# A two-layer transformer block on one core: normed rows for the expert gather, a new order of the last expert loads, and first slots that hold one contraction step

## The reference, cut to what matters

```python
def chunk(t):                                   # t: 128 tokens x 1024, already rmsnorm(x, g)
    grp_p = softmax(t @ w_grp + b_grp)          # 4 groups of 8 experts, best group
    e_p = softmax(logits of that group)         # best two experts in it
    combine = one_hot(expert) * weights         # tokens x 32
    a = einsum('cd,edf->cef', t, w_gate)
    u = einsum('cd,edf->cef', t, w_up)
    hid = silu(a) * u * combine[..., None]
    return einsum('cef,efd->cd', hid, w_down)
```

## Time and profile before

| | us |
|---|---|
| median of 3 runs | 1060.23 (1059.67 to 1060.28) |
| the profiled execution's own time | 1059.21 |
| its span, from first to last instruction | 1057.4 |
| PE busy | 1009.9 (96%) |
| DVE busy | 286.1 (27%) |
| ACT busy | 207.1 (20%) |
| HBM read | 288.44 MB, 275 GB/s over the span |

### The profile page before, as it was taken

One profiled execution on the slowest core, in us unless ns is written; L12 is line 12 of the kernel. 1 busy time (PEld: TensorE's weight loads), 2 busy tenths in 40 slices (PEclk: granted clock), 3 DMA queues, 4 the chain that ended last, 5 costly groups with the idle time before them and its releaser, 6 DMA issues. The chain is left out here.

```text
span 1057.4 us, 14177 instructions
## 1 busy us (share of the span) xinstructions
PE 1009.9 (96%) x5804; PEld 744.6 (70%) x5804; DVE 286.1 (27%) x985; ACT 207.1 (20%) x572; POOL 25.3 (2%) x72
## 2 busy tenths in 40 slices
PE   9999999999999999798899999999999999997795
PEld 8888788778887555444388887888888865553451
DVE  2321533442423211110131225344333331110102
ACT  1211344450010020000011105444300202000001
POOL 0000000000000000000010000000000000000000
PEclk9999999999999999989999999999999989998898
DMA  9956664437956999999996553443298569999995
GB/s 297 324 184 199 108 191 112 173 98 283 359 194 253 423 421 421 421 420 421 370 320 214 162 158 103 142 160 119 90 382 324 198 283 421 421 421 421 421 418 197
DMA packets 126424, 292.04 MB, mean 276 GB/s; under 512 B 13583, under 2 KB 84501, under 8 KB 104597
## 3 DMA queue, kind: packets, MB, share of 16 engines
q1 hardware_dynamic: 122992, 288.36, 73.6%
q10 hardware_dynamic: 3364, 2.74, 1.6%
HBM read 288.44 MB, written 2.64 MB: 275 GB/s over the span
## 5 line engine op out<-in xcount | busy, mean ns | idle before, releaser
L842 PE MATMUL bank<-tail,ring 128*128 128x256 f32 x1280 | 289.1, 382 | 0.0
L842 PEld LDWEIGHTS bank<-tail,ring 128*128 128x128 f32 x1280 | 239.2, 190 | 39.4 <-issue 8.7
L1642 PE MATMUL bank<-ring,tail 128*32 128x512 f32 x896 | 109.1, 643 | 25.6 <-DMA ring<-in_moe_w_up 21.8
L1615 PEld LDWEIGHTS bank<-tail,x_res 128*128 128x128 f32 x512 | 123.3, 335 | 13.1 <-issue 11.7
L1615 PE MATMUL bank<-tail,x_res 128*128 128x128 f32 x512 | 126.9, 408 | 1.1 <-DVE tail L1825 1.1
L1642 PEld LDWEIGHTS bank<-ring,tail 128*32 128x32 f32 x896 | 31.2, 117 | 100.6 <-issue 100.6
L1085 PE MATMUL bank<-tail,ring 128*128 128x256 f32 x384 | 83.4, 380 | 0.0
L1085 PEld LDWEIGHTS bank<-tail,ring 128*128 128x128 f32 x384 | 72.8, 190 | 10.2 <-issue 0.3
L1182 ACT ACTIVATE ring<-ring,small 128x128 f32<-128x128 f32 (+1 forms) x128 | 56.6, 443 | 75.0 <-DVE small L1429 75.0
L1892 DVE SCALAR_TENSOR_TENSOR tail<-tail,bank 128x256 f32<-128x256 f32 x16 | 6.7, 421 | 237.8 <-ACT tail L1760 237.8
L1710 PE MATMUL bank<-ring,tail 128*32 128x512 f32 x480 | 58.2, 595 | 4.6 <-DVE tail L1903 4.6
(11 more groups left out here) (276 smaller groups left out, 784.9 us busy)
## 6 DMA issues: line engine op xcount, KB each, us to landing
ring<-in_moe_w_gate SPq DMA_DIRECT2D x64, 1024.0 KB, 18.3
ring<-in_moe_w_up SPq DMA_DIRECT2D x64, 1024.0 KB, 20.3
ring<-in_moe_w_down SPq DMA_DIRECT2D x52, 1024.0 KB, 16.1
ring<-in_w_in SPq DMA_DIRECT2D x48, 1024.0 KB, 7.3
ring<-in_w_out SPq DMA_DIRECT2D x8, 1024.0 KB, 10.7
ring<-in_moe_w_down SPq DMA_DIRECT2D x16, 512.0 KB, 15.6
ring<-in_w_o_mla SPq DMA_DIRECT2D x4, 1024.0 KB, 5.2
ring<-in_w_o_fox SPq DMA_DIRECT2D x4, 1024.0 KB, 5.0
```

The source lines that it names most:

```text
L842: last = pe.matmul(dst, weight(k), hT[:, k, :], start=(k == 0), stop=(k == KD - 1))
L1615: last = pe.matmul(b[:, (k % 4) * P:(k % 4 + 1) * P], rows_k, Sel[:, g % 2, t, :], start=(t == 0 and k % 4 == 0), stop=(t == NT - 1), skip ...
L1642: last = pe.matmul(bank[4][CAP * e:CAP * e + CAP, :].rearrange("p (a f) -> p a f", a=2), XT[:, k, CAP * e:CAP * e + CAP], ring[:, lo:lo + ...
```

## The change

The second extra slot's space now holds `h2` first, the token rows in contraction order and multiplied by `rstd`, made by ACT (`normed_rows`). The gathers of groups 0 and 3 to 7 read `h2` as weights, in one run of 128 elements, with a plain 0/1 selection. Groups 1 and 2 (`RAW`) still gather from `x` with the scaled selection, since load 21 lies in `h2`'s space then; their output weights come from `W12`, which is divided by `rstd`. After group 1, `normed_rows` makes `h2` again. Load 21 is issued by `moe_sync` when both gathers of group 0 are done (`s_xg` 2).

Slots 0 to 7 each hold one contraction step, gate and up of four experts, and are filled by two loads of half the size. `first_gate_up` frees one slot a step.

The last 16 loads have another order: gate and up of group 7 are loads 80 to 87, the down matrices of group 6 are 88 to 91, those of group 7 stay 92 to 95. PE does `gate_up(7)` and `turn_hidden(7)` ahead of `down(6)` and its scatter. The hidden rows of group 7 are put into `Sel[:, 0]`. SP's wait before the next layer's first loads is on `gate_up(7)`. On DVE, two small operations of `route` (line 1791's and line 1803's) come behind the selection.

```diff
-    x0 = kept(2048, NT, KD, P)
+    h2 = kept(2048, NT, KD, P)
     EXTRA = [kept(4096, SLOT), kept(2048, SLOT)]
+    def item(c):
+        if c < LOADS - 16:
+            return divmod(c, 12)
+        return (NGRP - 1, c - (LOADS - 16)) if c < LOADS - 8 else (NGRP - 2 + (c >= LOADS - 4), 8 + c % 4)
+    def place(g, i):
+        if g == NGRP - 1 and i < 8:
+            return LOADS - 16 + i
+        return 12 * g + i + (8 if g == NGRP - 2 and i >= 8 else 0)
...
     def first_group_load(sp, layer, c):
-        j, i = divmod(c, 2)
-        src = A["moe_w_up" if i else "moe_w_gate"][layer, 0:4].rearrange("e (p k) f -> p e k f", k=KD)
-        sp.dma_start(ring[:, moe_slot(c), :].rearrange("p (e k f) -> p e k f", e=4, k=2),
-                     src[:, :, 2 * j:2 * j + 2, :]).then_inc(landed[moe_slot(c)], 16)
+        for i, name in enumerate(("moe_w_gate", "moe_w_up")):
+            src = A[name][layer, 0:4].rearrange("e (p k) f -> p e k f", k=KD)
+            sp.dma_start(ring[:, moe_slot(c), :].rearrange("p (e a f) -> p e a f", e=4, a=2)[:, :, i, :],
+                         src[:, :, c, :]).then_inc(landed[moe_slot(c)], 16)
...
                 sp.wait_ge(s_op, 5 + c - 16)
                 moe_load(sp, layer, c)
-            moe_load(sp, layer, 21)
...
+        RAW = (1, 2)
+        def hidden_rows(g):
+            return hidT if g < NGRP - 1 else Sel[:, 0]
...
         def moe_sync(sp):
+            sp.wait_ge(s_xg, 2)
+            moe_load(sp, layer, SLOTS + 1)
             for c in range(SLOTS + 2, LOADS - 4):
...
-                if g == 0 and i in (0, 2, 4, 6):
-                    sp.wait_ge(s_g0, i // 2 + 1)
+                if g == 0 and i < 8:
+                    sp.wait_ge(s_g0, i + 1)
...
             if layer + 1 < DEPTH:
-                sp.wait_ge(s_y, 2 * NGRP - 2)
+                sp.wait_ge(s_gu, NGRP - 1)
...
+                    weight = W12[:, t, 4 * gr - 4:4 * gr] if gr in RAW else Wsel[:, t, 4 * gr:4 * gr + 4]
...
             # gather
-                    rows_k = x[:, t, :].rearrange("p (q k) -> p k q", k=KD)[:, k, :]
+                    rows_k = x[:, t, :].rearrange("p (q k) -> p k q", k=KD)[:, k, :] if g in RAW else h2[:, t, k, :]
...
             pe.wait_ge(s_S, 1)
+            pe.wait_ge(s_h2, 1)
             gather(0, 0)
...
             pe.wait_ge(s_S, 2)
+            pe.wait_ge(s_h2, 2)
             gather(0, 1)
...
             # first_gate_up, for k in range(KD)
-                    if k % 2 == 0:
-                        moe_wait(pe, k)
-                        moe_wait(pe, k + 1)
+                    moe_wait(pe, k)
...
-                    if k % 2:
-                        last.then_inc(s_g0, 1)
+                    last.then_inc(s_g0, 1)
...
+            for g in range(NGRP):
...
+                if g == 0:
+                    first_gate_up()
+                else:
+                    gate_up(g)
+                if g + 1 < NGRP:
+                    pe.wait_ge(s_S, g + 3)
+                    if g + 1 == 3:
+                        pe.wait_ge(s_h2, 4)
+                    for t in range(NT):
+                        gather(g + 1, t)
+                turn_hidden(g)
+                if g < NGRP - 1:
+                    turn_weights(g)
+                if g < NGRP - 2:
+                    down(g)
+                    scatter_group(g)
+            down(NGRP - 2)
+            scatter_group(NGRP - 2)
+            turn_weights(NGRP - 1)
+            down(NGRP - 1)
+            scatter_group(NGRP - 1)
...
         # moe_scalar, behind the last sum of squares
+            def normed_rows():
+                for t in range(NT):
+                    act.wait_ge(s_rstd2, t + 1)
+                    act.activation(h2[:, t], x[:, t, :].rearrange("p (q k) -> p k q", k=KD), ACT.Copy,
+                                   scale=rstd[:, t:t + 1]).then_inc(s_h2, 1)
+            act.wait_ge(s_op, 8)
+            normed_rows()
...
                 if g == 1:
-                    for t in range(NT):
-                        act.activation(x0[:, t], x[:, t, :].rearrange("p (q k) -> p k q", k=KD), ACT.Copy)
+                    normed_rows()
...
         # pick_first
-                s(dve.tensor_tensor(picked(0)[:, t], places..., bc(Rk[:, t, 0:4], ...), ALU.is_equal))
-                s.sync()
-                dve.tensor_scalar(Sel[:, 0, t, :], Sel[:, 0, t, :], rstd[:, t:t + 1], None, ALU.mult).then_inc(s_S, 1)
+                dve.tensor_tensor(picked(0)[:, t], places..., bc(Rk[:, t, 0:4], ...), ALU.is_equal).then_inc(s_S, 1)
...
-            s(dve.tensor_tensor(rw[:, :, 5:6], rw[:, :, 5:6], rw[:, :, 7:8], ALU.mult))
-            s.sync()
...
+            dve.tensor_tensor(W12, Wsel[:, :, 4:12], bc(rw[:, :, 7:8]..., [P, NT, 8]), ALU.mult).then_inc(s_wsel, 1)
```

More of the change, by code:

```diff
@@ L294, in program @@
     cmax = tiny(940, 2)
+    W12 = tiny(942, NT, 8)
     ovf = sb("ovf", [P, 1], I32)
@@ L453, in in_extra @@
         return SLOTS <= c < SLOTS + 2
+    def item(c):
[6 more added lines that the diff above has]
+        return 12 * g + i + (8 if g == NGRP - 2 and i >= 8 else 0)
+    assert all(place(*item(c_)) == c_ for c_ in range(LOADS))
     def moe_home(c):
@@ new lines, in turn_hidden, with down @@
+            def turn_hidden(g):
+                pe.wait_ge(s_hd, g + 1)
+                for a in range(2):
+                    last = pe.transpose(bank[4][:, a * P:(a + 1) * P], hid[:, 1, a::2], ident)
+                last.then_inc(s_hdt, 1)
+            def down(g):
+                pe.wait_ge(s_hde, g + 1)
+                for i in range(8, 12):
+                    moe_wait(pe, place(g, i))
+                for n in range(2):
+                    if n == 1 and g + 1 < NGRP:
+                        pe.wait_ge(s_xge, 2 * g + 4)
+                    if n == 1 and g == NGRP - 1:
+                        pe.wait_ge(s_side, layer * 96 + 96)
+                    for a in range(2):
+                        for e in range(4):
+                            last = pe.matmul(bank[5 + n][CAP * e:CAP * e + CAP, :],
+                                             hidden_rows(g)[:, a, CAP * e:CAP * e + CAP],
+                                             moe_home(place(g, 8 + e))[:, a * D + 512 * n:a * D + 512 * n + 512],
+                                             start=(a == 0), stop=(a == 1))
+                    last.then_inc(s_y, 1)
@@ L1670, in moe_tensor, with scatter_group @@
+            def scatter_group(g):
+                pe.wait_ge(s_ste, g + 1)
+                for half in range(2):
+                    pe.wait_ge(s_ye, 2 * g + half + 1)
+                    for t in range(NT):
+                        last = scatter(g, t, half)
+                        if g == NGRP - 1:
+                            last.then_inc(s_fin, 1)
+                if g < NGRP - 1:
+                    last.then_inc(s_scat, 1)
             for g in range(NGRP):
@@ L1716, in moe_tensor @@
-                pe.wait_ge(s_ste, g + 1)
-                for half in range(2):
-                    pe.wait_ge(s_ye, 2 * g + half + 1)
-                    for t in range(NT):
-                        last = scatter(g, t, half)
-                        if g == NGRP - 1:
-                            last.then_inc(s_fin, 1)
-                if g < NGRP - 1:
-                    last.then_inc(s_scat, 1)
+                turn_hidden(g)
+                if g < NGRP - 1:
+                    turn_weights(g)
@@ L1750, in moe_scalar, with gate_tanh @@
             act.activation(rw[:, 1, 3:4], rw[:, 1, 2:3], ACT.Exp).then_inc(s_dex, 1)
-            for g in range(NGRP):
-                if g == 3:
-                    load_overflow(act)
+            def gate_tanh(g):
                 if g == 0:
-                    act.wait_ge(s_g0, KD // 2)
+                    act.wait_ge(s_g0, KD)
                 else:
```

109 lines of the change are left out of this document (50 added, 59 removed).

## The result

| | median, us | range | runs |
|---|---|---|---|
| before | 1059.95 | 1059.46 to 1060.28 | 4 |
| after | 1052.85 | 1050.76 to 1053.67 | 4 |

The ratio is 0.993, with a 95% interval of 0.9917 to 0.9943: 7.1 us off. The profiled execution of after is the slowest of its four, 1053.67 (span 1051.8), so the two profiles stand only 5.5 us apart.

What follows compares the result with a forecast made beforehand. Bound: when the DMA engines start their unbroken run, and PE's work after the last loads land. Tail gains of 4.7 and 4.8 us, head included, make 9.5; less 1.8 for clock, 7.7 off, so 1052.5 us; range 1049.5 to 1057.

Steps and rivals of the forecast that it cites:

- The head: Start of each expert stage: faster gathers let load 21 go out near 327.1, gaining 2.5 us in layer 0, 3.7 in layer 1.
- the bound: Expert stages: the end is set by the DMA run's start and PE's work after the last loads; work between is free.
- the last byte: Tail: last halves land 10.8 us after load 91, so down 7's second half starts 4.7 and 4.8 us earlier, head included.
- the clock: Tail: down 6 starting at half clock after waiting for load 91 loses 1.8 us, in one layer of the two.
- The gather's pace: Gathers at each expert stage's start: 0.115 us a record with weights in one run, 1.84 for 16, against 4.1 strided.
- Rival C: Gathers at the stage's start: no faster, as the strided read was not their limit; 1059 us, chance 0.05.
- rival B: Half clock in both tails, or in the gathers at the stage's start; 3 to 6 us off, 1054 to 1057, chance 0.20.
- The first slots: Loads of slots 0 to 7: 16 half-size ones take 2.4 us more, covered by a DMA pause, costed at nothing.
- Work in between: Middle of the stage: gathers 3 to 7 save 2.1 us a tile on PE, all under DMA's 29.9 a group; worth nothing.
- Rival B's head: Start of the expert stage: two gathers at half clock, 0.204 us a record, 2.9 a layer; within a rival of chance 0.20.
- Layer 1's take-up: Layer 1's first projection: starts at 527.6, 4.7 us earlier, with no wait for its loads, so the gain passes.

## Why the prediction was right, and where it was not

The forecast was 1052.5, and 1052.85 came. The head and the bound were read rightly. In the tail two terms of the 7.7 us were wrong, the last byte and the clock, and that their errors had opposite signs is luck. The next points say how much.

- **The gather's pace** was right: 2.02 to 2.05 us for 16 records, against 1.84 and the length of a last product. Rival C (the strided read was not its limit) is out. At half clock it is 3.37 to 3.63, rival B's 0.204 a record with a little on top.
- **The head.** The wait ahead of gather(0,0) was 0.99, predicted 1.1. Load 21 was predicted at 327.1: 327.06, 326.92, 326.86 and 326.72 in four heads of layer 0 at full clock. In layer 1, 844.59 stands 2.2 us later on the scale of before, where layer 1 began that much later: 846.8 against 847.0. The head's gain was put at 2.5 and 3.7; undoing it alone costs 4.7 in all by the medians and 3.0 by the profiles. Part of the difference is load 21, which costs 2.9 at the start of the run and not 2.49, some 0.4 a layer. Part is that with the old head the single steps of the first slots do help: counted from the first gather, load 22 went out 10.60 and 10.92 us later there, and 11.54 and 12.70 before.
- **The first slots** cost nothing, as predicted, and beside the new head they bring nothing either (1052.78 against 1052.87).
- **Work in between** was free, as predicted, as far as the waits show it: 49.0 us in place of 21.8. The prediction read the page's strip a little off: counted from one, it stands at 9 in slices 14 to 21 and 34 to 39. Nothing of the sum hangs on this.
- **The last byte** is the step that was mis-sized. It is what is late next, as predicted, but later. Load 91 came in time: where PE waits for it, at 1023.53, it is 180.42 after load 21; the prediction had 847.0 and 1027.3, so 180.3. The last halves took 12.2 us from there and not 10.8 (11.7 to 12.3 in ten of the twelve tails of the new order where down 6 waits for load 91; 10.7 and 10.9 in the two where load 91 itself came 1.3 and 1.5 us late). Counted from load 21, the prediction had the second half 191.6 and 190.5 us later (layer 1's from the old last byte, not by this sum), and it came 192.57 and 192.59 later: 1.0 and 2.1 us too good, 3.1 together. The gain beyond the head was put at 2.2 and 1.1 us by this; from load 22 on, the kernel with the old head and the new order shows 1.7 in layer 0 and none in layer 1.
- **The clock in the tail** was wrong in what it costs. The prediction's own figures, 1.7 to 2.7 of loss with 1.3 hidden, give 0.4 to 1.4 for a tail; it took 1.8, and no row gives that. A down 6 at half clock does occur, in 5 of the 14 profiled tails that have the new order and load 21 behind the gathers, and gate/up 7 is the slow one (8.77) in 8 more. The wait for the last halves hides both: it is 192.2 to 192.7 us from load 21 in all 14. The 1.8 us taken for it paid by chance for more than half of the last byte's 3.1. What the prediction did not look at is the product behind that wait, which nothing hides: in 4 of all 24 profiled tails of the new order it took 3.08 to 3.58 in place of 1.92, though in none of these 14.
- **Rival B's head** happened, in some executions: the first gather at half clock in 4 of the 14 heads profiled without warm-up products, 1.5 to 1.6 us each time. The profiled execution of after is one of them. Rival B had it in both gathers, 2.9 a layer; the second was always at full clock.
- **Layer 1's take-up** was right: its first projection waits for no load. It starts at 530.07, and at 528.59 with the head at full clock; predicted was 527.6, 1.0 too early as the last byte was.

By the profile at full clock in both heads the account closes to some tenths: 9.5 predicted for the two layers, less 3.1, is 6.4; its own time is 1059.21 - 1052.46 = 6.75 below before. With one gather at half clock it would be 4.8, and the first profile shows 5.5. The medians, with both kinds of execution in them, show 7.1 where 7.7 was forecast.

## What to carry to other kernels

Where a stage is one long queue of loads, as here, what counts is its first free issue and what PE does behind its last byte. Cut the head, then ask what is the first thing in the queue and whether it could have gone before it, as the tiles put apart and kept warm show (1049.32 for 1051.79 on the same chip). Price the last byte from a queue's end that the trace shows, not from its steady rate. A slow product that stands ahead of a longer wait costs nothing, and the same clock behind the last wait costs all it takes; so before a clock loss is charged, look at what the next instruction waits for. And compare a kernel with a yardstick from its own chip.

## What the runs showed of the hardware

- The same wait of 0.99 to 1.00 us among short products was followed by a first gather of 2.02 us in 10 heads and by one of 3.37 to 3.63 in 4, at a granted clock of 0.50 to 0.56 (1.2 GHz), in kernels that are the same there. With four warm-up products in its place it took 2.05 in all 10 heads profiled. Why one execution falls and another doesn't is open.
- In the 24 tails with the new order, gate/up 7 took 8.77 us behind its wait of 2.0 in 11 and 7.07 in 13. Down 6 took 4.99 to 5.34 in 7 of those 13, and 3.64 wherever gate/up 7 had been slow. The second half of down 7 took 3.08 to 3.58 in the 4 tails where PE had waited 2.48 to 2.90 us for it, and 1.92 or 1.93 in the 18 where it had waited 0.60 to 2.30.
- From the release of down 6 to that of the second half of down 7, 4.19 MB took 11.7 to 12.3 us in most tails, against 10.8 at the steady 387 GB/s. With nothing queued behind, the DMA share sinks over the last 2 us, and the waiting product is released 1 to 2 us after the last bytes (1038.22 in the windows above). Loads queued behind have no part in the delay (192.42 and 192.57 us with them held). What sets the gap stays open.
- A 128x1024 copy on ScalarE with a scale from a column (line 1785) takes 2.14 us (2.13 to 2.20), the plain one 2.05 (line 1770 before).
